# One load for the eight width marks, an announced jump at the end of the wide form, and a last mixer whose gate products are spread out

## The reference, cut to what matters

```
# experts: top 2 of 8, each a SwiGLU of width 3584
combine = sum(one_hot(top_i, 8) * gates)             # 256 x 8
for e in range(8):
    out = out + combine[:, e:e+1] * ((silu(t @ w1[e]) * (t @ w3[e])) @ w2[e])
# second block's mixer
z = rms_norm_2(x) @ w_in;  q, k, v, xr, yr = split(z)      # yr: 512 columns, the "gates"
lru_out = (rg_lru(xc, forward) + rg_lru(xc, backward)) * gelu(yr)
mixed = concat([block_attention(q, k, v), lru_out]) @ w_out
```

## Time and profile before

| | us |
|---|---|
| median of 3 runs | 2310.25 |
| lowest and highest run | 2308.36, 2311.13 |
| the profiled execution | 2302.45 |
| its span, first to last instruction | 2300.6 |
| PE busy | 2156.1 (94%) |
| DVE, ACT, POOL busy | 1392.5, 1108.7, 1180.7 |

### The profile page before, as it was taken

The page is one execution under the profiler, slowest core; times in us unless marked ns, Lnnn a source line. Parts: engine busy times, 40 slices in busy tenths (PEclk is TensorE's granted clock), DMA queues, the critical chain, the costliest instruction groups (busy, mean ns, idle before and its releaser), DMA issues.

```text
span 2300.6 us, 26818 instructions
## 1 busy us (share of the span) xinstructions
PE 2156.1 (94%) x10612; PEld 1729.5 (75%) x10612; DVE 1392.5 (61%) x1801; ACT 1108.7 (48%) x1111; POOL 1180.7 (51%) x465
## 2 busy tenths in 40 slices
PE   8999899989997899999999999999999996998997
PEld 7577588875685677777777777888777775758997
DVE  4565633365656577777777775443467777535665
ACT  1232243312331576767677674433367674444553
POOL 0120055401200698989899895555479894103543
PEclk9999899999998999999999999999999998989999
DMA  8200454522004698989999896555579896315560
GB/s 307 73 1 28 162 205 174 201 98 74 1 3 162 230 361 327 364 314 362 347 329 358 313 359 250 183 183 183 183 262 359 317 361 218 111 37 201 184 220 19
DMA packets 208095, 484.41 MB, mean 211 GB/s; under 512 B 9169, under 2 KB 13009, under 8 KB 207057
## 3 DMA queue, kind: packets, MB, share of 16 engines
q1 hardware_dynamic: 207952, 482.50, 57.8%
HBM read 481.44 MB, written 1.05 MB: 210 GB/s over the span
## 4 chain that ended last, share of the span: by engine, by line
PE 87%; DVE 7%; ACT 3%; issue 2%; POOL 1%; DMA 0%; DVEq 0%; ACTq 0%; SPq 0%; POOLq 0%
PE bank L957 21%; PE bank L959 20%; PE bank L958 20%; PE bank L594 12%; PE bank L786 5%; PE bank L601 3%; PE bank L747 1%; DVE b_arena L1338 1%; DVE b_X L1338 1%; ACT e_hi L2210 1%; PE bank L703 1%; PE bank L864 1%; PE bank L1221 1%; POOL e_lo L2759 1%; DVE b_arena L1344 1%
## 5 line engine op out<-in xcount | busy, mean ns | idle before, releaser
L2759 POOL TENSOR_TENSOR e_lo<-b_ring,e_hi 128x512 fp32r<-128x512 f32 (+1 forms) x401 | 1122.7, 2821 | 636.3 <-ACT e_hi L2210 636.3
L1810 DVE TENSOR_TENSOR e_lo<-b_ring,e_hi 128x1536 fp32r<-128x1536 f32 (+2 forms) x407 | 782.0, 1922 | 480.6 <-ACT e_hi L2210 479.3
L2210 ACT ACTIVATE e_hi<-b_ring 128x2048 fp32r<-128x2048 f32 (+1 forms) x407 | 777.2, 1912 | 336.5 <-PE bank L959 330.5
L957 PE MATMUL bank<-e_hi,e_xh 128*128 128x512 f32 (+1 forms) x1200 | 476.6, 397 | 33.6 <-issue 15.7
L959 PE MATMUL bank<-e_hi,e_xl 128*128 128x512 f32 (+1 forms) x1200 | 467.3, 389 | 0.0
L958 PE MATMUL bank<-e_lo,e_xh 128*128 128x512 f32 (+1 forms) x1200 | 467.0, 389 | 0.0
L957 PEld LDWEIGHTS bank<-e_hi,e_xh 128*128 128x128 f32 x1200 | 227.1, 189 | 100.4 <-issue 52.6
L957 PE MATMUL bank<-e_hi,e_th 128*128 128x512 f32 x688 | 272.4, 396 | 0.7
L958 PE MATMUL bank<-e_lo,e_th 128*128 128x512 f32 x688 | 268.5, 390 | 0.0
L959 PE MATMUL bank<-e_hi,e_tl 128*128 128x512 f32 x688 | 268.3, 390 | 0.0
L959 PEld LDWEIGHTS bank<-e_hi,e_xl 128*128 128x128 f32 x1200 | 226.9, 189 | 48.2
(11 more groups left out here) (234 smaller groups left out, 2316.0 us busy)
## 6 DMA issues: line engine op xcount, KB each, us to landing
b_ring<-in_moe_w SPq DMA_DIRECT2D x168, 2048.0 KB, 8.1
b_ring<-in_w_in SPq DMA_DIRECT2D x15, 2048.0 KB, 8.7
b_ring<-in_ffn_w SPq DMA_DIRECT2D x15, 2048.0 KB, 7.8
b_ring<-in_w_up SPq DMA_DIRECT2D x12, 2048.0 KB, 7.8
b_ring<-in_w_down SPq DMA_DIRECT2D x6, 2048.0 KB, 8.7
b_ring<-in_w_o SPq DMA_DIRECT2D x4, 2048.0 KB, 7.7
b_gain<-in_gains SPq DMA_DIRECT2D x6, 1024.0 KB, 4.8
b_ring<-in_w_out SPq DMA_DIRECT2D x2, 2048.0 KB, 8.3
```

The source lines that it names most:

```text
L957: e.matmul(out, ah, bh, start=first, stop=False)
L1810: e.tensor_tensor(lo[:, 0:at], raw[:, 0:at], r32(hi[:, 0:at]), ALU.subtract).then_inc(lo_dve.sem)
L2210: return e.activation(out, x, ACT.Copy)
L2759: e.tensor_tensor(lo[:, at:], raw[:, at:], r32(hi[:, at:]), ALU.subtract).then_inc(lo_pool.sem)
```

## The change

The PE stream reads the eight marks with one call that loads all of them, without the check of their bounds. In the wide form a second hint is placed, at the turning step with u == 6, for the unconditional jump at the form's end. In the last mixer the three halves of the gates that were made in steps 0, 1 and 2 of the attention are made in steps 0, 3 and 5.

```
-            def expert(ex, tiles, wide, hints):
+            def expert(ex, tiles, wide, hints, on):
 ...
                 def aside(kind, u, hf):
                     if more and kind == "T" and u == 3:
                         hints.append(e.mark_branch_hint_location(hint=wide[ex + 1]))
+                    if tiles == 2 and kind == "T" and u == 6:
+                        on.append(e.mark_branch_hint_location())
 ...
-                wide = [e.to_reg(e.value_load(flag[0:1, ex:ex + 1], min_val=0, max_val=1)) for ex in range(NE)]
+                wide = [e.to_reg(v) for v in nc.values_load_multi_w_load_instructions(flag[0:1, 0:NE], [e.engine], min_val=0, max_val=1,
+                                                                                           skip_runtime_bounds_check_because="a comparison gives 0 or 1")[1]]
 ...
                     with nc.body(f"wide{ex}", valid_engines=[e.engine]):
-                        expert(ex, 2, wide, hints)
-                        e.br(f"done{ex}")
+                        on = []
+                        expert(ex, 2, wide, hints, on)
+                        end = e.br(f"done{ex}")
+                        for place in on:
+                            end.branch_hint(place)
                     with nc.body(f"narrow{ex}", valid_engines=[e.engine]):
-                        expert(ex, 1, wide, hints)
+                        expert(ex, 1, wide, hints, [])
                         e.br(f"done{ex}")
 ...
                 for i in range(11):
                     if i < 8:
                         scores(i)
-                        next(gates, None)
+                        if i in (0, 3, 5):
+                            next(gates, None)
```

## The result

The changed kernel is faster: 2300.5 us against 2307.1, medians of 20 runs each, ratio 0.9974 with a 95% interval of 0.9966 to 0.9982. That is 6.0 us, 4.2 to 7.8. (The two medians differ by 6.5; the ratio is estimated from all runs.) The forecast was 10.8 us less, 2299.5.

What follows compares the result with a forecast made beforehand. PE was taken as the bound (87% of the chain), idle on issue at expert 0 and behind wide expert 5. Terms -4.3 - 0.9 - 5.3 - 2.5 + 2.2 = -10.8 took 2310.25 to 2299.5 us; range over cases 2293.5 to 2308.5.

Steps and rivals of the forecast that it cites:

- The reads: Ahead of expert 0: one unchecked load of about 1.0 us replaces eight checked reads, so PE starts earlier, -4.3 us.
- the bound for a load of 2.4 us: Ahead of expert 0: if the load cost eight median single loads, 2.4 us, the reads would gain only -2.8.
- six per us: At expert 0: PE's assumed product rate, by which 24 products on two pieces last until the third is wanted, from 761.4.
- The clock at expert 0: At expert 0's start: the shorter gap of 3.4 us saves half of the low clock's 1.9 us cost, -0.9.
- The rule by gaps: Between experts: the clock stays up after a PE gap of 2.34 us and falls after one of 3.16 us.
- The jump: At wide expert 5's end: the announced jump takes 0.3 in place of 6.17 and PE starts expert 6 earlier, -5.3 us.
- The clock behind the wide expert: At expert 6's start: the gap shrinks to 1.4 us, so the low clock's whole cost is saved, -2.5.
- The gates: Last mixer's attention: step 5's half costs +3.4 at low clock, less 1.2 given back, together +2.2 us.
- two chances in three of one: Last mixer: the dense half regains one step at the upper clock, worth up to 1.8 us, with that chance; -1.2.
- the clock answers: Rival, last mixer: spread gates keep or lift the clock for the attention's rest, -3.4 in place of +2.2; chance 0.15.
- its own sign of being wrong: Last mixer: the prediction is wrong if the attention's low-clock stretch of 20.4 us becomes much shorter or longer.

Runs made afterwards that it cites:

- e8: Changed kernel with the next expert's branch announced directly before it, where the jump lands, and no longer early in the wide form; 2293.9 us, executed once.
- e4: Changed kernel without the jump: each form ends in the next expert's branch itself, announced at the turning step with u == 3; 0.9971 of the kernel before.
- e2: Kernel before with the announced jump at the wide form's end alone; ratio 0.9997 (0.9983 to 1.0011).
- e6: Changed kernel with no announcement of the next expert's branch in the wide form; 2302.5 us, executed once.
- e11: Kernel before with the halves of the gates in steps 0, 4 and 6 of the last mixer's attention; 2308.4 us, executed once.

## Why the prediction was right in sum, and wrong in four of its five terms

**The reads** were right: -4.3 forecast, 4.4 less in the two profiles, and one load of 0.78 where 1.0 was taken. From the gathering to the first product, which also holds the varying branch, it is 5.1 less by the averages over the kernels (9.6 us in seven kernels, 14.8 in six). Two slips did no harm: the bound for a load of 2.4 us is -2.9, not -2.8; and products at the upper level start 0.23 us apart, so PE makes 4.4 of them in a us. The "six per us" counts those that only reach into the stretch, and the third pieces were wanted 1.4 us later than the prediction says. The Trainium skill ("Runtime: NRT & Kernel Launch", Instruction fetch mechanics) gives about 200 ns for each register, an estimated 1.6 us for eight; the measured load is half of that.

**The clock at expert 0** had the wrong sign. I took half of 1.9 as saved. The clock fell all the same in six of the seven kernels with one load, and in most of them PE, which now starts earlier, works through more of the low stretch. In the same six it falls again at expert 1, where the gap is the old 2.34; of the seven kernels with eight loads one does that. From expert 0's first product to the gathering of expert 5 the kernels with one load took 652.8 us on average and those with eight checked reads 651.5: 1.3 us lost, not 0.9 gained. The single values overlap (649.0 to 653.8 against 650.6 to 653.9), so the sign is likely and not certain. The rule by gaps that the term rests on, 2.34 harmless and 3.16 harmful, does not hold either: in e8 the clock stayed up from 756.4 to 1664.4, behind that gap of 3.16 too.

**The jump.** It was announced and short, as forecast, and the step that failed is the next one: "Whether that one takes 0.34 or again 3.46 makes no difference: it ends by 1665.5". There was a third case. The branch took 7.35 and ended 4 us later than that bound. So the -5.3 were -2.0 from line 1081 to expert 6's first product (10.32 to 8.36). The reasoning is right once the jump is gone: in e4 PE starts when the sums are in, 6.7 us after line 1081.

**The clock behind the wide expert** (-2.5 forecast) was mostly lost with it. The gap of 2.99 is followed by a low stretch in the changed kernel as well (1669.6 to 1673.0), of which PE works through 2.8 us in place of 4.9; up to expert 7 that gained 1.1. Over the kernels even this is not steady: from line 1081 to expert 7 it took 140.05 us on average with the announced jump and the long branch (the changed kernel, e2, e6, e8) and 142.05 with the unannounced jump (seven kernels). So both terms together, -7.8 in the forecast, are -2.0.

**The gates** had the wrong sign: +2.2 forecast, 2.5 less. The work moved as described: the half of step 3 ahead of idle time, that of step 5 at half speed, 3.78. The term that failed is what it gives back, "two chances in three of one" step. The clock rose 1.1 us behind the half and stayed up to the output products, and the following steps ran in about 2.8 us (from the scores of 2028.68 to those of 2031.49) in place of 5.07. This is the rival "the clock answers", with a chance of 0.15, at a size of 2.5 where it said 3.4. The prediction also named its own sign of being wrong, an attention with a low stretch much shorter than 20.4 us, and that sign came: 10.2.

**The sum.** By the averages over the kernels: -5.1 for the reads, +1.3 for the clock behind them, -2.0 at the wide expert's end up to expert 7, -2.4 in the mixer, together -8.2; measured were 4.2 to 7.8 less. The stage behind the mixer brings it inside: 241.2 us on average in the seven kernels with the halves in steps 0, 3 and 5, and 240.4 in the five without a late half, +0.8, so -7.4. Other places that no edit touches vary as much: the time up to the gathering for expert 0 was 747.6 to 754.5 us over the fourteen profiles, and the stage behind expert 7 about 125.5 or 127. That the forecast of 10.8 less ended at the right time is luck twice over: its errors, 5.8 too much behind the wide expert and 4.7 too little in the mixer, went opposite ways, and the median that it started from was 3.2 too high.

## What to carry to other kernels

One load of eight values took 0.78 us, a load of one 0.30 to 0.50, and the check of each value another 0.30: where PE waits for a branch, read all the marks at once, and unchecked if a comparison made them. Announce a branch only where no taken jump stands between the announcement and it; better, end each alternative in the next branch itself, for here a jump made short ahead of a branch lost most of its gain to that branch. When a stage of thin products runs at the lower clock, put spare dense work inside it and not ahead of it, and read from the trace whether the clock answers: here it did, where the forecast had allowed for less than one step of it.

## What the runs showed of the hardware that was not expected

- A branch met right after an announced jump takes 7.3 us, against 3.0 to 3.5 after an unannounced one of 6.0 to 6.5. Announced late it takes 6.0 to 6.2, and 0.4 with no jump between.
- Announcements hold long: 116 us in e4, nearly half of the wide expert's time. The Trainium skill ("Runtime: NRT & Kernel Launch", Instruction fetch mechanics) calls prefetch purely sequential; the 0.32 and 0.38 us of announced branches against 6.2 and 3.5 of others disagree.
- Within about 1.2 us of the end of a dense half of 3.6 to 3.8 us at the lower level the clock rose in all eight kernels that had it in step 5 (and in e11, which had it in step 4), and the thin steps behind it kept the upper level, which they had not regained by themselves in 20 us.
- The same gap of 2.34 us between experts met the upper level in some profiles and was followed by a low stretch of 3.4 us in others, with nothing changed around it; behind the gap of 3.16 us the clock fell in thirteen profiles of fourteen.
